# Sliding-window attention in units of four heads instead of one, in a two-layer hybrid decoder step on one core

## The reference, cut to what matters

```python
s = jnp.einsum('bnqkgd,bnskd->bnkgqs', qr, kb).astype(f32) * hd ** -0.5
...
s = jnp.where(mask[None, :, None, None], s, -jnp.inf)
sink = sinks.astype(f32).reshape(n_kv, grp)[None, None, :, :, None, None]
m = jnp.maximum(jnp.max(s, axis=-1, keepdims=True), sink)
e = jnp.exp(s - m)
p = e / (jnp.sum(e, axis=-1, keepdims=True) + jnp.exp(sink - m))
o = jnp.einsum('bnkgqs,bnskd->bnqkgd', p.astype(v.dtype), vb).reshape(bsz, seq, n_q * hd)
```

## Time and profile before

| what | value |
|---|---|
| time, median of 3 runs (lowest to highest) | 3127.86 us (3121.34 to 3130.57) |
| time of the profiled execution | 3128.77 us |
| its span, first to last instruction | 3127.0 us |
| mean granted TensorE clock over the span | 0.908 |
| busy share of the span: PE, DVE, ACT | 87%, 42%, 29% |
| stage `swa_attend`, from its first VectorE instruction to the first product of `odd_out` | 2242.70 to 2345.25 us |

### The profile page before, as it was taken

How to read it: one execution, slowest core, us unless ns; L and a number is a source line. 1 busy time by engine, 2 the same in 40 slices (tenths; PEclk the granted TensorE clock), 3 DMA queues, 4 the chain that set the end, 5 groups by cost and what they waited for, 6 DMA issues and landing times. The chain is left out here.

```text
span 3127.0 us, 49964 instructions
## 1 busy us (share of the span) xinstructions
PE 2722.8 (87%) x20579; PEld 2579.9 (83%) x20579; DVE 1314.5 (42%) x1792; ACT 892.9 (29%) x1151; POOL 171.7 (5%) x143
## 2 busy tenths in 40 slices
PE   6999989859486788999989999988598667899998
PEld 6999989848475668999989999986458665899998
DVE  6434443251334434434436334346453444443342
ACT  4412221120424324412234212131332432342121
POOL 0000000000000000000028000050000000000000
PEclk9999999965788889999999999998658888999999
DMA  3222322310134242322222222220103414222222
GB/s 113 90 78 88 93 63 86 96 27 4 54 105 164 67 148 68 90 78 87 93 75 88 88 78 88 82 66 16 49 1 93 163 67 162 74 87 88 81 86 84
DMA packets 76355, 258.82 MB, mean 83 GB/s; under 512 B 9780, under 2 KB 19204, under 8 KB 75232
## 3 DMA queue, kind: packets, MB, share of 16 engines
q1 hardware_dynamic: 75728, 255.81, 25.9%
q0 software_dynamic: 528, 1.64, 0.2%
HBM read 246.85 MB, written 10.57 MB: 82 GB/s over the span
## 5 line engine op out<-in xcount | busy, mean ns | idle before, releaser
L96 DVE TENSOR_TENSOR w_low<-w_raw,w_high 128x1024 fp32r<-128x1024 f32 (+2 forms) x360 | 470.6, 1307 | 1277.1 <-ACT w_high L92 1276.7
L307 PE MATMUL ps<-h_high,w_high 128*128 128x272 f32 x4192 | 889.2, 294 | 119.3 <-DVE h_low L256 65.3
L307 PE MATMUL ps<-h_high,w_low 128*128 128x272 f32 x4192 | 880.8, 292 | 0.0
L307 PE MATMUL ps<-h_low,w_high 128*128 128x272 f32 x4192 | 879.6, 292 | 0.0
L92 ACT ACTIVATE w_high<-w_raw 128x1024 fp32r<-128x1024 f32 (+2 forms) x360 | 399.9, 1112 | 1444.9 <-PE ps L307 1340.0
L307 PEld LDWEIGHTS ps<-h_high,w_high 128*128 128x128 f32 x4192 | 675.3, 193 | 127.1 <-DVE h_low L256 67.4
L307 PEld LDWEIGHTS ps<-h_low,w_high 128*128 128x128 f32 x4192 | 674.9, 193 | 0.0
L307 PEld LDWEIGHTS ps<-h_high,w_low 128*128 128x128 f32 x4192 | 668.8, 193 | 0.0
L307 PE MATMUL ps<-ffn_hid,w_high 128*128 128x272 f32 x2816 | 475.3, 291 | 24.7 <-PEq L149 24.7
L307 PEld LDWEIGHTS ps<-ffn_hid,w_high 128*128 128x128 f32 x2816 | 403.7, 191 | 26.2 <-issue 26.2
L307 PE MATMUL ps<-ffn_hid,w_low 128*128 128x272 f32 x1408 | 294.9, 291 | 0.0
(11 more groups left out here) (372 smaller groups left out, 2038.7 us busy)
## 6 DMA issues: line engine op xcount, KB each, us to landing
w_raw<-in_ffn_w_gate SPq DMA_DIRECT2D x88, 512.0 KB, 3.5
w_raw<-in_ffn_w_up SPq DMA_DIRECT2D x88, 512.0 KB, 3.5
w_raw<-in_ffn_w_down SPq DMA_DIRECT2D x64, 704.0 KB, 4.1
mem_ring<-in_cache_mem_k SPq DMA_DIRECT2D x32, 512.0 KB, 5.9
mem_ring<-in_cache_mem_v SPq DMA_DIRECT2D x32, 512.0 KB, 6.4
w_raw<-in_even_w_in SPq DMA_DIRECT2D x26, 512.0 KB, 3.5
w_raw<-in_mem_w_k SPq DMA_DIRECT2D x16, 512.0 KB, 3.6
w_raw<-in_mem_w_v SPq DMA_DIRECT2D x16, 512.0 KB, 3.5
```

Of the source, the lines that this page charges most:

```text
L96: return nc.vector.tensor_tensor(core.low[s][:, 0:kt * P], core.raw[s][:, 0:kt * P], core.high[s][:, 0:kt * P].bitcast(F32), ALU.subtract)
L307: last = nc.tensor.matmul(acc[s][:, a, :], w, x[:, k, a * width:(a + 1) * width], start=(k == 0 and n == 0), stop=(k == kt - 1 and n == 2))
```

## The change

A unit becomes one query block and one key group with its four heads: 8 units, and one sample unit for both key groups in place of two. The core of the diff (SyncE's block, which issues the same 13 DMAs, the declarations of semaphores, and the sample products are left out):

```diff
-        units = [(b, i, kv) for b in range(NB) for i in range(4) for kv in range(2)]
+        units = [(b, kv) for b in range(NB) for kv in range(2)] + ["sample"]
...
-        logit = sb("logit", [P, 2, 2 * P])
-        prob = sb("prob", [P, 3, 2 * P])
-        pT = sb("pT", [P, 2, 2, P])
+        prob = sb("prob", [P, 3, 4, 2 * P])
+        pT = sb("pT", [P, 2, 4, P])
...
-        o_sb = sb("o_sb", [P, 4, TOK])
...
-                        if u >= 3:
-                            pe.wait_ge(S["masked"], u - 2)
-                        nc.tensor.matmul(scores_at(u)[:, 0:keys(u)], pr[r, SQ + i, b * P:(b + 1) * P],
-                                         kT[r, lo:(b + 1) * P], start=True, stop=True).then_inc(S["scored"], 1)
+                        s = scores_of(u)
+                        if u >= 2:
+                            pe.wait_ge(masked, u - 1)
+                        for i in range(4):
+                            ins = nc.tensor.matmul(s[:, i], pr[r, SQ + i, b * P:(b + 1) * P], kT[r, lo:(b + 1) * P],
+                                                   start=True, stop=True)
+                        ins.then_inc(scored, 1)
...
-                        if u >= 2:
-                            pe.wait_ge(S["turn_copied"], u - 1)
+                        if u == 0:
+                            pe.wait_ge(sT_ready, 2)
+                        else:
+                            pe.wait_ge(turn_copied, u)
...
-                            ins = nc.tensor.transpose(core.ps[0:w, 2 + u % 2, t * P:(t + 1) * P],
-                                                      prob[:, u % 3, t * P:t * P + w], core.mats[:, IDENT])
+                            for i in range(heads_of(u)):
+                                ins = nc.tensor.transpose(core.ps[0:w, 4 + t, i * P:(i + 1) * P],
+                                                          prob[:, u % 3, i, t * P:t * P + w], core.mats[:, IDENT])
...
-                            ins = nc.tensor.matmul(core.ps[r, 4 + (u // 2) % 2, 0:P],
-                                                   v_tok[:, b - nt + 1 + t, 0, r], pT[:, u % 2, t, :],
-                                                   start=(t == 0), stop=(t == nt - 1))
+                            ins = nc.tensor.matmul(core.ps[r, out_bank(u), :], v_tok[:, b - nt + 1 + t, 0, r],
+                                                   pT[:, t].rearrange("p h c -> p (h c)"), start=(t == 0), stop=(t == nt - 1))
...
+                    def low(b):
+                        dve.wait_ge(high_ready, b + 1)
+                        c = slice(b * P, (b + 1) * P)
+                        nc.vector.tensor_tensor(core.h[1][:, 4:8, c], core.ps[:, 6 + b % 2, :].rearrange("p (i c) -> p i c", c=P),
+                                                core.h[0][:, 4:8, c].bitcast(F32), ALU.subtract).then_inc(low_ready, 1)
...
-                    dve.wait_ge(S["high_ready"], 4)
-                    nc.vector.tensor_tensor(core.h[1][:, 4:8], o_sb[:], core.h[0][:, 4:8].bitcast(F32), ALU.subtract)
...
                     def turned_copy(u):
+                        act.wait_ge(turned, u + 1)
+                        if u >= 1:
+                            act.wait_ge(out_done, u)
```

More of the change, by code:

```diff
@@ new lines, in window_attention, with heads_of, scores_of @@
+            out_done, high_ready, low_ready, q_ready, cached, sT_ready, stored = [sem(n) for n in
+                ("out_done", "high_ready", "low_ready", "q_ready", "cached", "sT_ready", "stored")]
+            def heads_of(u):
+                return 2 if u == SAMPLE else 4
+            def keys(u):
+                if u == SAMPLE:
+                    return P + TS
+                return 2 * P if units[u][0] else P
+            def scores_of(u):
+                bank = 2 * (u % 2)
+                if u == SAMPLE:
+                    return core.ps[:, bank:bank + 2, 0:P + TS]
+                s = core.ps[:, bank:bank + 2, :].rearrange("p k (h c) -> p (k h) c", c=2 * P)
+                return s[:, :, 0:keys(u)]
@@ new lines, in prob_of, with row, minus_sinks_of, out_bank @@
+            def prob_of(u):
+                return prob[:, u % 3, 0:heads_of(u), 0:keys(u)]
+            def row(k, u):
+                return small[:, k, u, 0:heads_of(u)]
+            def minus_sinks_of(u):
+                if u == SAMPLE:
+                    return minus_sinks[:, 8:10]
+                kv = units[u][1]
+                return minus_sinks[:, 4 * kv:4 * kv + 4]
+            def out_bank(u):
+                return 6 + (u // 2) % 2
+            def cached_at(kv):
+                return core.ps[:, 4 + kv, 0:P]
@@ L1826, in sample_values @@
[L1826 to L1837 removed]
+                        ins.then_inc(cached, 1)
@@ new lines, in sample_scores @@
+                    def sample_scores():
+                        s = scores_of(SAMPLE)
+                        pe.wait_ge(masked, SAMPLE - 1)
+                        for kv in range(2):
+                            r = slice(64 * kv, 64 * kv + 64)
+                            nc.tensor.transpose(s[:, kv, 0:P], sT[:, kv, :], core.mats[:, IDENT])
+                            ins = nc.tensor.matmul(s[:, kv, P:P + TS], qs[r, :], kT[r, SEQ:TOK], start=True, stop=True)
+                        ins.then_inc(scored, 1)
@@ L1892, in _ @@
+                    dve.wait_ge(q_ready, 4)
+                    soft(0)
                     for kv in range(2):
-                        dve.wait_ge(S["cached"], kv + 1)
-                        nc.vector.tensor_copy(sT[:, kv], cached_at(kv)).then_inc(S["sT_ready"], 1)
-                    for u in range(NU + 2):
+                        dve.wait_ge(cached, kv + 1)
+                        nc.vector.tensor_copy(sT[:, kv], cached_at(kv)).then_inc(sT_ready, 1)
+                    for u in range(1, NU):
@@ L1896, in _ @@
                         soft(u)
-                        if u >= 1:
-                            divide(u - 1)
-                    divide(NU + 1)
-                    dve.wait_ge(S["high_ready"], 4)
-                    nc.vector.tensor_tensor(core.h[1][:, 4:8], o_sb[:], core.h[0][:, 4:8].bitcast(F32), ALU.subtract)
+                        divide(u - 1)
+                        if u >= 5 and u % 2:
+                            low((u - 5) // 2)
+                    divide(SAMPLE)
+                    for b in range(2, NB):
+                        low(b)
@@ L1945, in _ @@
[L1945 to L1952 removed]
+                        act.wait_ge(sink_shifted, u + 1)
@@ new lines, in high @@
+                    def high(b):
+                        act.wait_ge(out_done, 2 * b + 2)
+                        nc.scalar.activation(core.h[0][:, 4:8, b * P:(b + 1) * P],
+                                             core.ps[:, 6 + b % 2, :].rearrange("p (i c) -> p i c", c=P), ACT.Copy
+                                             ).then_inc(high_ready, 1)
+                    exps(0)
+                    for u in range(1, NU):
+                        exps(u)
+                        turned_copy(u - 1)
+                        if u >= 4 and u % 2 == 0:
+                            high((u - 4) // 2)
```

220 lines of the change are left out of this document (94 added, 126 removed).

## The result

The changed kernel took 3085.95 us (median of 4 runs, 3073.74 to 3086.61) beside 3128.36 us for the kernel before on the same chip: a ratio of 0.986, 95% interval 0.983 to 0.989. In a second measurement of the same two kernels it was 0.987 (0.985 to 0.990). The forecast was 3109, the range ended at 3086; what came is its first rival, the clock that rises, which had a chance of 0.27.

What follows compares the result with a forecast made beforehand. TensorE at its lower clock (0.50) was taken to bound the stage `swa_attend`. Terms -16.3 - 2.1 + 3.6 - 4.0 = -18.8 us, from the profiled 3128.77 to 3110.0, less 0.9 for the median: 3109; range 3086 to 3117.

Steps and rivals of the forecast that it cites:

- The joined step at 0.50: TensorE's line: fixed 0.68 us paid once for four heads, later unit 9.24 against 11.28 us; eight units, -16.3 us.
- Rival 2: Weight loads show in each of a unit's four scores products: 7.0 us less gain, 3116 us; chance 0.10.
- The start: Cached products and unit 2's scores cover unit 0's softmax, for which TensorE had waited: -2.1 us.
- VectorE, ScalarE: Per step VectorE needs 4.9 us and ScalarE 3.9 of TensorE's 9.24, priced by twin operations; both hide under TensorE.
- rival 1: Stage's clock rises from 0.50 to 1.00, step 5.4 us, VectorE's 4.9 beside it: 20 us more gain, 3089; chance 0.27.
- The single buffers: At the stage's end, both last `turn`s wait about 1.3 us each, the sample's values about 1.0: +3.6 us.
- The tail: From the last product's end to the end of the low part: 5.3 us becomes 1.3, -4.0 us.
- PEclk stays 0.50 in all of it: Expected profile of the changed stage: clock at 0.50 throughout, stage about 84 us.

Runs made afterwards that it cites:

- broken-up order: Changed kernel with the same instructions reordered on TensorE, single scores and value products alternating, no long succession on 128 rows: 0.993, 3107.4 us, stage 77.66 us.
- the run with narrow values: Changed kernel with each value product of 512 columns made as four of 128 columns: 0.985, 3086.2 us, stage 58.90 us.
- the changed kernel with added products: Changed kernel with seven products whose result nobody reads added ahead of the stage: 0.986, stage 58.86 us.
- the one try: Kernel before with seven products whose result nobody reads added ahead of the stage, to enter it at 1.00: 0.999, stage 102.11 us.

## Why the forecast was wrong, step by step

- **The joined step at 0.50: right.** Scores 3.71, transposes 1.89 and 1.90 for a value product by itself stand where 3.7, 1.9 and 3.6 for two in a row were put. Rival 2 is out: four scores products in a row on the same 64 rows take their streaming and one 0.29. The Trainium skill, page TensorE: Matmul & The Clock Gate, section Part 3: Packing small matmuls, lets a weight load overlap, in its list of what overlaps, only where the row group differs; the measurement decides against that here.
- **The start: right.** A wait of 0.34 us is left of 2.1.
- **VectorE, ScalarE: right in price.** 1.22 and 1.02 us as the twins. At 1.00 VectorE's step is 4.51 us (L1895 at 2278.28 and 2282.79) under TensorE's 4.81: it is nearly the bound, as rival 1 had it.
- **The single buffers: right.** 1.26, 1.26 and 0.79 are 3.3 us where 3.6 was put; a wait of 0.38 for VectorE, at 1.00, was not in the sum.
- **The tail: right,** shown by itself (4.04 us).
- **"PEclk stays 0.50 in all of it": the step that failed.** The sum put a rise at nothing; the level rose near 2275.6 and the stage took 62.62 us where about 84 were forecast. From 2275.96 to the end of the last product at 2301.80 are 25.8 us with 3.7 of waits. The other 22.1 would be 1.90 times as long at 0.50 (scores and transposes, 5.60 to 2.95): about 19.9 us more, by that estimate. A stage without the rise would then be 82.5 us. By the same estimate the change itself brought 20.0 us where the sum said 18.8, and the rise another 19.9.
- **The rival's price came out, in part by luck; its chance was too low.** It said 20 us for six steps less most of the first, with the step at 5.4 us where it is 4.81 to 4.85, and the step in which the rise comes was a guess. In the trace the rise came late: only two of the six groups of 256-key scores ran at 1.00, and the rest of the gain is that of the transposes and value products of the last units and of the sample. Its 3089 becomes 3086 with the 2.2 us ahead of the stage and 1.07 behind it, which no step of the forecast brought. The reason given against it was that scores and values still use half of the array, as before. That lumped together two halves: scores use 64 rows, values 128 rows and 64 columns. The runs show that the 64 rows of the scores matter; what the 64 columns of the values do was not tried. With the scores put on 128 rows, the kernel before left 0.50 with nothing joined, and the broken-up order did too; with 64-row scores between every two groups it did not. The prediction had read the 14.4 us of 32-row products at 0.50 as speaking of any product on half of the array.

Theory A stands in this form: in this stage, with TensorE nearly without a gap, the level follows what the products are and in which succession they come. For the rows of the scores this is shown: in three orders, with TensorE's order and columns left alone, 128 rows in place of 64 shortened the stage from 102.55 to 77.64, from 77.66 to 61.26 and from 62.62 to 54.00 us. That the new order rose because eight transposes and the value products of four heads stand together is shown in part: broken up into single groups it stayed at 0.50, but with the transposes set apart it still rose, later, at the end of a pair of value products, and did not keep the level. The Trainium skill's same page, section Why this matters for your kernels, advises to keep TensorE busy for the upper level; here a TensorE that was busy 10.00 of 10 us stayed at 0.50, so in this stage that was not enough.

Open: why the rise came some 27 us into the stage in the run with narrow values and in the changed kernel with added products, both in the scores behind eight transposes and one value product, while in two traces of the changed kernel the same group passed without it and the next one, at 35 us, raised it. And whether the kernel before would hold 1.00 if it kept it past the entry, since the one try lost it half a microsecond into the cached scores.

## What to carry to other kernels

Where a stage shows TensorE fully busy at 0.50, ask first what its products use before cutting instructions: zeros that put 64-row products on 128 rows cost two copies and two zeroings on ScalarE, and took 24.9 us off the stage here, while the change without the rise is put at some 20 by the estimate above. When an edit groups small products into long runs, price the sum at both levels of the clock and let the chances follow the rows used and the order, not TensorE's busy share. And once the clock is up, look for the next bound: here VectorE's step was 4.51 us under TensorE's 4.81.

## What the runs showed of the hardware that was not expected

- TensorE's busy share does not tell its level: 0.50 throughout 60 us of the broken-up order, 58.8 of them busy; 1.00 in most of the same order with scores on 128 rows, where it was busy for 3.75 of 4 us.
- Over 16 products of 16 columns (32 records) the level fell, with 64 rows (near 2244.9 us) as with 128 rows (near 2253.6 us), TensorE's column reading busy; over 8 of them, 1.7 us at 1.00, it did not.
- Behind a standstill of 1.99 us the level fell half a microsecond into the stage's first products, behind one of 1.95 us within 0.1 us of them; in a standstill of 4.74 us it fell ahead of them.
- Scores on 128 rows with half zeros take the same time as on 64 rows (1.99 us for four products of 256 columns at 1.00, on either).
